# Ten pairs of gate and up tiles of two feed-forward layers as seven half-size block products each

## The reference

```python
def swiglu(x, wi, wo):                       # wi: 1024 x 5632, wo: 2816 x 1024
    gate, up = jnp.split(x @ wi, 2, axis=-1)
    return (jax.nn.silu(gate) * up) @ wo
# layer li of the first block
h = h + 0.5 * swiglu(rms_norm(h, ffn1_norm[li]), ffn1_wi[li], ffn1_wo[li])
hn = rms_norm(h, mix_norm[li])
h = h + (gla_pool_mixer(hn, ...) if li % 2 == 0 else dsa_mixer(hn, ...))
h = h + 0.5 * swiglu(rms_norm(h, ffn2_norm[li]), ffn2_wi[li], ffn2_wo[li])
```

## Time and profile before

| | us |
|---|---|
| three timed runs, median | 2774.28 (2774.22 to 2774.34) |
| the profiled execution | 2774.09 |
| span of its instructions | 2772.4 |
| PE busy | 2724.8 (98%), 14196 matmuls |
| DVE busy | 1577.9 (57%) |
| ACT busy | 1200.2 (43%) |
| POOL busy | 624.0 (23%) |

### The profile page before, as it was taken

How to read it: one execution, slowest core, us unless ns; L and a number is a source line. 1 busy time by engine, 2 the same in 40 slices (tenths; PEclk the granted TensorE clock), 3 DMA queues, 4 the chain that set the end, 5 groups by cost and what they waited for, 6 DMA issues and landing times.

```text
span 2772.4 us, 39098 instructions
## 1 busy us (share of the span) xinstructions
PE 2724.8 (98%) x14196; PEld 2211.8 (80%) x14196; DVE 1577.9 (57%) x2453; ACT 1200.2 (43%) x1804; POOL 624.0 (23%) x607
## 2 busy tenths in 40 slices
PE   8999999999999999999989999999999999899998
PEld 6888888788888888887778888877888888777777
...
DMA packets 484826, 255.23 MB, mean 92 GB/s; under 512 B 17843, under 2 KB 478422, under 8 KB 484710
## 3 DMA queue, kind: packets, MB, share of 16 engines
...
q10 hardware_dynamic: 176, 0.27, 0.0%
...
## 4 chain that ended last, share of the span: by engine, by line
PE 91%; DVE 5%; ACT 1%; issue 1%; POOL 1%; DMA 0%; SPq 0%; DVEq 0%; ACTq 0%; POOLq 0%
PE bank L259 73%; PE bank L1879 2%; PE bank L1910 1%; PE bank L1912 1%; PE bank L1911 1%; DVE w_lo L245 1%; DVE dsa_work L1577 1%; PE bank L1986 1%; DVE small L1575 1%; PE bank L2794 1%; PE bank L2786 1%; PE bank L2023 1%; PE bank L2819 1%; DVE gdn_blocks L2383 1%; PE bank L981 1%
## 5 line engine op out<-in xcount | busy, mean ns | idle before, releaser
L259 PE MATMUL bank<-x_hi,w_hi 128*128 128x512 f32 x2320 | 939.7, 405 | 8.0 <-DVE w_lo L245 4.2
L259 PE MATMUL bank<-x_hi,w_lo 128*128 128x512 f32 x2320 | 907.7, 391 | 0.0
L259 PE MATMUL bank<-x_lo,w_hi 128*128 128x512 f32 x2320 | 907.1, 391 | 0.6 <-DVE x_lo L586 0.6
L245 DVE TENSOR_TENSOR w_lo<-w_raw,w_hi 128x1024 fp32r<-128x1024 f32 x429 | 531.6, 1241 | 551.5 <-ACT w_hi L239 550.9
L239 ACT ACTIVATE w_hi<-w_raw 128x1024 fp32r<-128x1024 f32 x429 | 450.7, 1055 | 621.2 <-PE bank L259 572.0
L259 PEld LDWEIGHTS bank<-x_hi,w_hi 128*128 128x128 f32 x2320 | 436.9, 188 | 107.7 <-issue 16.8
L259 PEld LDWEIGHTS bank<-x_hi,w_lo 128*128 128x128 f32 x2320 | 436.5, 188 | 93.4
L259 PEld LDWEIGHTS bank<-x_lo,w_hi 128*128 128x128 f32 x2320 | 437.5, 189 | 89.0 <-issue 5.5
L435 POOL TENSOR_TENSOR sumsq<-sumsq,sq 128x512 f32<-128x512 f32 x56 | 92.3, 1649 | 1291.5 <-ACT sq L421 1290.9
L259 PE MATMUL bank<-h_hi,w_hi 128*128 128x512 f32 x768 | 298.9, 389 | 1.6 <-DVE h_lo L1610 1.6
L259 PE MATMUL bank<-h_hi,w_lo 128*128 128x512 f32 x768 | 298.8, 389 | 0.0
...
## 6 DMA issues: line engine op xcount, KB each, us to landing
w_raw<-in_ffn_wi_dram SPq DMA_DIRECT2D x176, 512.0 KB, 3.8
w_raw<-in_ffn_wo_dram SPq DMA_DIRECT2D x64, 512.0 KB, 4.1
w_raw<-in_ada_w_dram SPq DMA_DIRECT2D x48, 512.0 KB, 4.9
w_raw<-in_a_w_in_dram SPq DMA_DIRECT2D x48, 512.0 KB, 3.9
w_raw<-in_b_w_in_dram SPq DMA_DIRECT2D x32, 512.0 KB, 4.1
...
w_raw<-in_even_w_in_dram SPq DMA_DIRECT2D x16, 512.0 KB, 4.0
w_raw<-in_a_w_out_dram SPq DMA_DIRECT2D x16, 512.0 KB, 3.4
```

What stands on the lines that cost most here:

```text
L245: dve.tensor_tensor(w_lo[s][:], w_raw[raw_of(b) % RAW][:], w_hi[s][:].bitcast(F32), ALU.subtract).then_inc(w_lo_done, 1)
L259: mm = pe.matmul(out, lhs[:, w], rhs(kt), start=first and kk == 0 and m == 0, stop=last and kk == len(kts) - 1 and m == 2)
```

## The change

`SEVEN = (0, 1)`, `SEVEN_AT, SEVEN_N = 4, 10`: in the first two feed-forward layers pairs 4 to 13 are computed in another way; pairs 0 to 3 and 14 to 21 stay. A gate block and its up block are seen as a 2 x 2 matrix of blocks (rows: gate, up; columns: inputs 0 to 511, inputs 512 to 1023), x as a 2 x 2 matrix too (inputs by tokens 0 to 255 and 256 to 511). The product of the two takes seven products of such blocks in place of eight. Each of the seven is 4 slices x 3 = 12 matmuls of 128x256 (`seven_group`).

What stands beside them: four sums of quarters of x, made once for a layer (`parts_act` scales x by the gain into `x_part`, `parts_pool` adds on GpSimd, `parts_hi` and `parts_lo` split). For every pair four sums of 128x512 on GpSimd: `both`, `three`, `low`, `all`; five splits in place of two (`left`, `both`, `all` of 512 columns, `row` and `low` of 1024); on the banks six VectorE instructions of 256 columns and two ScalarE copies of 256 columns (`copy_act`) in place of two VectorE ones of 512. Silu, product, `h_hi` and `h_lo` stay, at 512 columns, one pair later. TensorE's order interleaves two pairs: groups 1 and 2 of pair n (`row`), then the last group of pair n-1 (`last_pe`, slot `all`), then two groups of pair n+1 (`left`, `both`), then two of pair n (`low`). A pair's raw blocks are loaded two pairs ahead (`seven_sp`), when the sums and splits that read the buffers are done. The code of these ten pairs is written out, not looped.

```diff
 OUT3 = 3
+
+SEVEN = (0, 1)
+SEVEN_AT, SEVEN_N = 4, 10
...
+            if f in SEVEN:
+                for o in range(AHEAD, 2 * SEVEN_AT):
+                    own(o)
+                for n in range(SEVEN_N + 2):
+                    at = (SEVEN_AT + n) * P
+                    seven_sp(sp, f, n, lambda m: weight_cols(wi, slice(m * FF + at, m * FF + at + P)))
...
-            if not ada_of(f):
+            if f in SEVEN:
+                def one(u, i=0, n=0, part=None):
+                    if not part:
+                        pe.wait_ge(tile_free, t0 + u + 1 + i * n)
+                    products(pe, b0 + u, bank[(t0 + u) % BANKS][:], x_of(x_hi), x_of(x_lo), range(KT), True, True, i, n, part)
+                project_pe(pe, run, b0, t0, 4, r, begun)
+                for u in range(4, 2 * SEVEN_AT - 1):
+                    one(u)
+                first_and_seventh_pe(pe, f, 0, 1)
+                seven_pe(pe, f, one)
+                o = 2 * (SEVEN_AT + SEVEN_N)
+                for u in range(1, 4):
+                    one(o + u)
+                with pe.Fori(1, (2 * FT - o) // 4) as i:
+                    for u in range(4):
+                        one(o + u, i, 4)
+            elif not ada_of(f):
                 project_pe(pe, run, b0, t0, 2 * FT, r, begun)
             else:
...
+        def seven_sp(sp, f, n, src):
+
+            raw = raw_of(seven_block(f, n))
+            c = seven(f) + n - 2
+            for m in range(2):
+                if n >= 2:
+                    if m == 0:
+                        sp.wait_ge(all_added, c + 1)
+                        sp.wait_ge(row_lo, c + 1)
+                    else:
+                        sp.wait_ge(low_lo, c + 1)
+                else:
+                    sp.wait_ge(w_lo_done, raw + m + 1)
+                dst = w_raw[(raw + m) % RAW].rearrange("p (k c) -> p k c", c=P)
+                sp.dma_start(dst, src(m)).then_inc(w_loaded[(raw + m) % RAW], 16)
+
+        def parts_act(act, f, gain):
+
+            for k in range(KT):
+                act.activation(x_part[:, k * T:k * T + T], hres[:, k * T:k * T + T], ACT.Copy, scale=gain[:, k:k + 1]).then_inc(part_made, 1)
...
+        PARTS = ((1, T2), (0, T2), (0, T1), (1, T1))
+
+        def parts_pool(pool, f):
+
+            c = 4 * SEVEN.index(f)
+            b11, b12, b21, b22 = (quarter(x_part, k, t) for k in range(2) for t in (T1, T2))
+            pool.wait_ge(part_made, KT * (SEVEN.index(f) + 1))
+            pool.tensor_tensor(b22, b22, b12, ALU.subtract).then_inc(part_added, 1)
+            pool.tensor_tensor(b12, b11, b12, ALU.subtract).then_inc(part_added, 1)
+            pool.wait_ge(part_added, c + 1)
+            pool.tensor_tensor(b11, b22, b11, ALU.add).then_inc(part_added, 1)
+            pool.wait_ge(part_added, c + 3)
+            pool.tensor_tensor(b21, b11, b21, ALU.subtract).then_inc(part_added, 1)
...
+        def seven_group(pe, slot, h, x, out, first=False):
+
+            hi, lo = w_hi[slot], w_lo[slot]
+            x_h, x_l = x
+            for k in range(4):
+                w = slice(h * T + k * P, h * T + k * P + P)
+                for m, (lhs, rhs) in enumerate(((hi, x_h), (hi, x_l), (lo, x_h))):
+                    mm = pe.matmul(out, lhs[:, w], rhs[:, k, :], start=first and k == 0 and m == 0, stop=k == 3 and m == 2, skip_group_check=True)
+            return mm
...
+        def first_and_seventh_pe(pe, f, n, which):
+            c = seven(f) + n
+            A, B = seven_banks(f, n)
+            if which == 1:
+                if n >= 2:
+                    pe.wait_ge(first_taken, c - 1)
+                    pe.wait_ge(last_joined, c - 1)
+                else:
+                    pe.wait_ge(tile_free, seven_tile(f, n) + 1)
+                pe.wait_ge(left_lo, c + 1)
+                seven_group(pe, slot_of(f, 1), 1, own_pair(0, T1), A[:, T1], True).then_inc(p1_done, 1)
+            else:
+                if n == 0:
+                    pe.wait_ge(part_lo, 4 * SEVEN.index(f) + 4)
+                pe.wait_ge(both_lo, c + 1)
+                seven_group(pe, slot_of(f, 2), 0, part_pair(0), A[:, T2]).then_inc(p7_done, 1)
+
+        def last_pe(pe, f, n):
+            c = seven(f) + n
+            pe.wait_ge(all_lo, c + 1)
+            pe.wait_ge(last_joined, c + 1)
+            pe.wait_ge(tile_free, BANKS + seven_tile(f, n) + 1)
+            seven_group(pe, slot_of(f, 1), 0, own_pair(1, T2), seven_banks(f, n)[1][:, T1]).then_inc(p3_done, 1)
+
+        def seven_pe(pe, f, one):
+            one(7, part=0)
+            first_and_seventh_pe(pe, f, 0, 7)
+            one(7, part=1)
+            for n in range(SEVEN_N):
+                c = seven(f) + n
+                A, B = seven_banks(f, n)
+                pe.wait_ge(row_lo, c + 1)
+                pe.wait_ge(p1_copied, c + 1)
+                seven_group(pe, slot_of(f, 0), 0, part_pair(2), B[:, T1])
+                pe.wait_ge(p7_copied, c + 1)
+                seven_group(pe, slot_of(f, 0), 1, own_pair(1, T1), A[:, T1]).then_inc(p2_done, 1)
+                if n:
+                    last_pe(pe, f, n - 1)
+                if n + 1 < SEVEN_N:
+                    first_and_seventh_pe(pe, f, n + 1, 1)
+                    first_and_seventh_pe(pe, f, n + 1, 7)
+                pe.wait_ge(low_lo, c + 1)
+                pe.wait_ge(p7_joined, c + 1)
+                seven_group(pe, slot_of(f, 3), 0, part_pair(1), B[:, T1])
+                seven_group(pe, slot_of(f, 3), 1, part_pair(3), B[:, T2]).then_inc(p4_done, 1)
+            pe.sem_inc(block_done, 2 * SEVEN_N)
+            o = 2 * (SEVEN_AT + SEVEN_N)
+            one(o, part=0)
+            last_pe(pe, f, SEVEN_N - 1)
+            one(o, part=1)
...
+        def left_act(act, f, n):
+            b = seven_block(f, n)
+            act.wait_ge(*loaded(raw_of(b)))
+            if n:
+                act.wait_ge(p1_done, seven(f) + n)
+            else:
+                act.wait_ge(block_done, b - 3 + SPLIT + 1)
+            act.activation(w_hi[slot_of(f, 1)][:, RIGHT_H], w_raw[raw_of(b) % RAW][:, LEFT_H], ACT.Copy).then_inc(left_hi, 1)
...
+        def row_act(act, f, n):
+            c, b = seven(f) + n, seven_block(f, n)
+            act.wait_ge(three_added, c + 1)
+            if n:
+                act.wait_ge(p2_done, c)
+            else:
+                act.wait_ge(block_done, b - 4 + SPLIT + 1)
+            act.activation(w_hi[slot_of(f, 0)][:], w_raw[raw_of(b) % RAW][:], ACT.Copy).then_inc(row_hi, 1)
...
+        def all_act(act, f, n):
+            c = seven(f) + n
+            act.wait_ge(all_added, c + 1)
+            if n:
+                act.wait_ge(p3_done, c)
+            act.activation(w_hi[slot_of(f, 1)][:, LEFT_H], w_all[:], ACT.Copy).then_inc(all_hi, 1)
+
+        def copy_act(act, f, n):
+            A, B = seven_banks(f, n)
+            act.wait_ge(p7_done, seven(f) + n + 1)
+            act.wait_ge(tile_free, seven_tile(f, n) + 2)
+            act.activation(B[:, T1], A[:, T1], ACT.Copy).then_inc(p1_copied, 1)
+            if n >= 2:
+                act.wait_ge(last_joined, seven(f) + n - 1)
+            act.activation(p7_copy[n % 2], A[:, T2], ACT.Copy).then_inc(p7_copied, 1)
...
+                    act.sem_inc(w_hi_done, 2 * SEVEN_N)
+                    next_hi(act, f, 0)
+                all_act(act, f, n)
+                if n:
+                    seven_silu(act, f, n - 1)
+                if n + 2 < SEVEN_N:
+                    left_act(act, f, n + 2)
+                if n + 1 < SEVEN_N:
+                    copy_act(act, f, n + 1)
+                if n:
+                    seven_h_hi(act, f, n - 1)
+                if n + 1 < SEVEN_N:
+                    low_act(act, f, n + 1)
+                if n + 2 < SEVEN_N:
+                    both_act(act, f, n + 2)
+            next_hi(act, f, 1)
+            seven_silu(act, f, SEVEN_N - 1)
+            next_hi(act, f, 2)
+            seven_h_hi(act, f, SEVEN_N - 1)
+            next_hi(act, f, 3)
...
+        def last_dve(dve, f, n):
+
+            s = (SEVEN_AT + n) % 2
+            A, B = seven_banks(f, n)
+            dve.wait_ge(p4_done, seven(f) + n + 1)
+            dve.tensor_tensor(prod[s][:, T2], B[:, T1], p7_copy[n % 2], ALU.add).then_inc(last_joined, 1)
+            dve.scalar_tensor_tensor(prod[s][:, T1], B[:, T2], -1.0, rstd[:, T1], ALU.mult, ALU.mult).then_inc(tile_free, 1)
+
+        def join_dve(dve, f, n):
+
+            s = (SEVEN_AT + n) % 2
+            A, B = seven_banks(f, n)
+            dve.wait_ge(p2_done, seven(f) + n + 1)
+            dve.wait_ge(p7_copied, seven(f) + n + 1)
+            dve.tensor_tensor(B[:, T2], B[:, T1], p7_copy[n % 2], ALU.add).then_inc(p7_joined, 1)
+            dve.tensor_tensor(gate_s[s][:, T1], A[:, T1], rstd[:, T1], ALU.mult).then_inc(first_taken, 1)
...
+            left_dve(dve, f, 0)
+            up(0)
+            product(0)
+            both_dve(dve, f, 0)
+            low(0)
+            row_dve(dve, f, 0)
+            gate(1)
```

(79 more changed lines are left out.)

191 lines of the change are left out of this document (186 added, 5 removed).

## The result

The changed kernel takes 2794.07 us (median of 4 runs, 2793.42 to 2794.40), the kernel before 2774.25 (4 runs, 2773.70 to 2774.34): ratio 1.0070, 95% interval 1.0057 to 1.0083. It is 0.7% slower; 2769.5 was forecast, in a range up to 2787. The profiled execution took 2793.42, its span 2791.5.

The account below looks back on a forecast made before the run. TensorE, 91% of the chain, was taken as the bound, with VectorE's turn setting the new pace. 2774.1 - 5.6 (twenty pairs) - 1.2 (slack per layer) + 2.2 (start stall) = 2769.5 us; 8-in-10 range 2751 to 2787.

Parts of the forecast that it names:

- The start of a layer: Before block 4: TensorE stalls 2.2 us in the first layer, none in the second; quarter sums and splits hidden beside blocks 4 to 7.
- A wait costs its own length: Unstated assumption in the sum: TensorE's 2.2 us stall at the layer start was added as 2.2 us.
- TensorE's pace: In the seven groups of a pair: 0.115 us per 256-column matmul, 9.66 us a pair; bounds 0.106 and 0.120.
- VectorE's turn: Steady pairs: VectorE's queue takes 10.6 us a pair with GpSimd's sums against 10.88 before; 9.0 us without them.
- the 0.9 forecast: Steady pairs: TensorE idles once a pair, 0.9 us before `last_pe`, waiting for VectorE's `last_dve`.
- The hold of 1.04: GpSimd's weight sums: each blocks VectorE instructions with two SBUF inputs for 1.04 of its 1.28 us; both engines take turns.
- TensorE sets the pace: Rival for the steady pairs: GpSimd's sums fit beside VectorE's work, turn under 9.66 us, time 2751.9 us; chance 0.22.
- The whole-instruction hold: Rival for the steady pairs: a sum blocks VectorE for its whole 1.28 us, turn 11.5 us, time 2788.7 us; chance 0.20.
- Matmuls at 0.13: Rival on TensorE: long runs of 256-column matmuls take 0.13 us each, 10.9 us a pair, about 2776 us; chance 0.08.
- The end of the ten pairs: After the last pair: half a block, 2.7 us, lies before `last_pe`, enough for a `last_dve`; no cost counted.

Follow-up runs that it names:

- 2: Changed kernel with the four quarter sums of activations per layer cut to 8 of 256 columns (output not the reference's); 2784.21 us.
- 6: Changed kernel with a new layer start: ScalarE's scaled copies later, quarter sums on VectorE, quarter splits around pair 0's left split; 2784.33 us.
- experiment 9: Kernel with weight and quarter sums on VectorE and early scaled copies, plus eleven extra low splits behind layer 1's last pair; 2781.09 us.
- experiment 4: Changed kernel with only VectorE's queue reordered: `h_lo` made one step later, behind the operation that frees the bank; 2792.12 us.
- 13: Kernel with all sums on VectorE, early scaled copies and bank copy first: pair 1's left and both splits moved ahead of other work; 2768.72 us.
- 5: Changed kernel with each pair's four weight sums moved from GpSimd to VectorE, spread over its turn; 2778.65 us.
- 7: Changed kernel with both the weight sums on VectorE and the new layer start with quarter sums on VectorE; 2767.31 us.
- experiment 1: Changed kernel with GpSimd's weight sums cut to 8 columns, some first ones kept whole (output not the reference's); 2779.28 us.
- experiment 10: Kernel with weight and quarter sums on VectorE and early scaled copies: one of four weight sums a pair put back on GpSimd; 2772.60 us.

## Why the forecast was wrong, step by step

- **The start of a layer** failed: 2.2 us, with "the four sums of quarters ... and their eight splits lie beside blocks 4 to 7". Block 4's wait was right (1.73, and nothing in layer 2; the terms given for it add up to 2.0, not 2.2). The cover wasn't there: the sums kept VectorE from the splits of blocks 4 and 5, and the eight quarter splits stood in both queues ahead of pair 0's left split. 14.5 us of waits in place of 2.2, 1.9 for their restarts and 4.0 of clock on top: 18.2 of the 24.6 us between forecast and result (1.4 more are the last section's, 0.6 stay unplaced). Experiments 2 and 6 show each part. I had worked out the length of this work (10 us on GpSimd) and not placed it, though I did so for the steady turn.
- **A wait costs its own length** was taken silently. The windows and experiment 9 show 1.7 to 2.3 us more for waits of 3.21, 4.60 and 10.94 us, and in all traces at hand each wait of 3.2 us and more in the two layers has the clock at half behind it. Below that it goes either way: 1.84 (experiment 4), 2.88, 2.93 (13) and 2.98 (2) have it, 1.73, 2.04 (5), 2.44 (6), 2.64 (7) and 2.90 (changed kernel) don't. So experiment 9 bears out its theory for a long wait, and not from 2 us on.
- **TensorE's pace**: 0.115 a matmul forecast, two in a row; 84 of them take 10.08 us in experiments 1 and 7, 0.120, the upper bound given. Alone it cost nothing, since VectorE's turn was longer; it caps what the idea can give at 16 us for twenty pairs.
- **VectorE's turn**: 10.6 forecast, 11.00 measured. As it binds in seven of ten turns only, the pairs saved about 2.4 us in place of 6.8: 4.4 of the 24.6. The mechanism is as described: the four steps named have 1.02 to 1.77, bank operations 0.41, one wait a pair before `last_pe`, released by `last_dve`. That this wait, 0.92 with its restart, is the 0.9 forecast is luck: both turns were forecast 0.4 too short. Without sums it would be TensorE's, as forecast (experiment 1). The size was off by 0.4: four sums cost 2.5 us here and 3.2 where VectorE has no idle time, against about 1.6 in my layout; the rest of the turn was 8.5 against 9.0.
- **The hold of 1.04** was too short. In the rows of the steady turn a VectorE step that begins beside a running sum is longer by what is left of the sum, less 0.14: 0.72 of 0.86 (left split at 120.00, sum until 120.86), 1.09 of 1.22 (product), 0.33 of 0.46 (`h_lo`), 0.40 of 0.54 (low split). All 75 such meetings in the changed kernel's trace give 0.135 to 0.153, and those of experiments 4 and 10 too. So a sum holds the way until 0.14 before its end, up to 1.14 of its 1.28, about the 1.13 from which the prediction has a turn pass 10.88. What it costs, 0.3 to 1.1, depends on how far it had got: 0.8 on average (experiment 4), 0.92 in experiment 10. In that one VectorE's steps went first three times; turns were not taken one by one. (`up_dve`, L1146, counted among the six on banks, has both inputs in SBUF; none of this hangs on it.)
- **Rivals.** TensorE sets the pace: no, 0.92 over it. The whole-instruction hold, 11.5 to 12.2 us: not in the turn, 11.00; the hold of 1.14 lies between the forecast's 1.04 and its 1.28. Its sign and its 2788.7 were nearer than the forecast; most of that nearness is luck, as the loss came from the start. The page of the Trainium skill that I weighed (SBUF — State Buffer, Who interferes with whom) calls the shared port pair an exclusive lock. The traces agree but for the last 0.14 us: the same low split was lengthened by 0.40 where 0.54 us of the sum were left, and by 1.08 where 1.22 were (experiment 4). Matmuls at 0.13: no.
- **The end of the ten pairs** cost nothing, as counted.
